# Two accumulators instead of one in the 31-tap depthwise convolution of the last block

## What is computed

```python
D_MODEL, SEQ, CONV_WIDTH, D_CONV_2 = 2048, 512, 31, 1024

def conformer_conv(glu_a, glu_b, conv_w, conv_b, ln_g, ln_b, w_pw, b_pw):
    u = glu_a * jax.nn.sigmoid(glu_b)
    u = lax.conv_general_dilated(
        u, conv_w.reshape(CONV_WIDTH, 1, D_CONV_2).astype(u.dtype),
        window_strides=(1,), padding=[(CONV_WIDTH - 1, 0)],
        dimension_numbers=('NWC', 'WIO', 'NWC'), feature_group_count=D_CONV_2) + conv_b
    u = jax.nn.silu(layer_norm(u, ln_g, ln_b))
    return u @ w_pw + b_pw
```

## Time and profile before

| | before |
|---|---|
| median of 3 runs | 3659.15 us (3657.35 to 3663.39) |
| profiled execution, its own time | 3659.0 us |
| span of its profile | 3657.4 us |
| PE, DVE, ACT, POOL busy | 94%, 60%, 36%, 6% of the span |
| line 1844 (taps 1 to 30), x240 | 180.5 us busy, 752 ns each, 35.9 us idle before |
| stretch 2822 to 3110 us | PE 263.7 us busy, DVE 249.3 us, granted PE clock 0.96 of full |

### The profile page before, as it was taken

How to read it: one execution, slowest core, us unless ns; L and a number is a source line. 1 busy time by engine, 2 the same in 40 slices (tenths; PEclk the granted TensorE clock), 3 DMA queues, 4 the chain that set the end, 5 groups by cost and what they waited for, 6 DMA issues and landing times.

```text
span 3657.4 us, 48550 instructions
## 1 busy us (share of the span) xinstructions
PE 3419.7 (94%) x16800; PEld 2707.4 (74%) x16800; DVE 2195.0 (60%) x2852; ACT 1319.3 (36%) x1757; POOL 210.7 (6%) x396
## 2 busy tenths in 40 slices
PE   8699998899999999998799999999998998998996
PEld 2299998678777777788688777777875777787784
DVE  6455545787676764666564565655655888444433
ACT  0144553432344433325522344443226212344323
POOL 1000000001000000110010000000110000000000
PEclk9799999999999999998899999999999999999998
DMA  9844445445222321654454233322652222221231
GB/s 379 278 161 170 164 152 212 150 169 204 109 100 106 106 98 72 230 208 145 178 205 173 104 112 108 108 96 72 222 191 93 91 80 92 78 78 63 101 120 66
DMA packets 95164, 516.32 MB, mean 141 GB/s; under 512 B 11536, under 2 KB 11568, under 8 KB 55760
## 3 DMA queue, kind: packets, MB, share of 16 engines
q1 hardware_dynamic: 51328, 343.95, 25.8%
q0 software_dynamic: 43728, 170.91, 13.6%
HBM read 492.80 MB, written 22.02 MB: 141 GB/s over the span
## 4 chain that ended last, share of the span: by engine, by line
PE 69%; DVE 13%; DVEq 5%; ACT 4%; issue 4%; DMA 4%; ACTq 1%; SPq 0%; POOL 0%; POOLq 0%; PEldq 0%
PE acc L995 19%; PE acc L997 19%; PE acc L996 19%; DVE xy L1844 5%; PE pv L1075 2%; DVE w_lo L1372 2%; PE S L1056 2%; DVEq L1843 2%; DVE gates L1419 2%; PE S L1234 2%; DVEq L1408 2%; PE misc L1216 1%; ACT w_hi L540 1%; PE S L1064 1%; ACT h_hi L540 1%
## 5 line engine op out<-in xcount | busy, mean ns | idle before, releaser
L995 PE MATMUL acc<-h_hi,w_hi 128*128 128x512 f32 (+1 forms) x4736 | 1752.6, 370 | 140.0 <-DVE h_lo L1378 67.3
L997 PE MATMUL acc<-h_hi,w_lo 128*128 128x512 f32 (+1 forms) x4736 | 1712.8, 362 | 0.0
L996 PE MATMUL acc<-h_lo,w_hi 128*128 128x512 f32 (+1 forms) x4736 | 1712.5, 362 | 0.0
L995 PEld LDWEIGHTS acc<-h_hi,w_hi 128*128 128x128 f32 x4736 | 909.1, 192 | 330.0 <-issue 121.8
L997 PEld LDWEIGHTS acc<-h_hi,w_lo 128*128 128x128 f32 x4736 | 909.3, 192 | 135.4
L996 PEld LDWEIGHTS acc<-h_lo,w_hi 128*128 128x128 f32 x4736 | 910.7, 192 | 130.8 <-issue 6.7
L1372 DVE TENSOR_TENSOR w_lo<-raw,w_hi 128x2048 fp32r<-128x2048 f32 x296 | 677.7, 2290 | 434.1 <-ACT w_hi L540 427.7
L540 ACT ACTIVATE w_hi<-raw 128x2048 fp32r<-128x2048 f32 x296 | 565.0, 1909 | 7.6 <-DVEq L1363 6.2
L540 ACT ACTIVATE ev<-acc 128x512 f32<-128x512 f32 (+1 forms) x210 | 111.1, 533 | 977.3 <-PE acc L997 951.9
L1419 DVE SCALAR_TENSOR_TENSOR gates<-gates,csil 128x512 f32<-128x512 f32 x568 | 412.4, 750 | 78.5 <-DMA gates<-in_wm 42.2
L540 ACT ACTIVATE work<-S,small 128x768 f32<-128x768 f32 (+1 forms) x160 | 129.2, 814 | 276.4 <-DVE small L1509 276.4
(11 more groups left out here) (199 smaller groups left out, 2053.4 us busy)
## 6 DMA issues: line engine op xcount, KB each, us to landing
raw<-in_w SPq DMA_DIRECT2D x296, 1024.0 KB, 4.8
gates<-in_wm POOLq DMA_DIRECT2D x216, 512.0 KB, 4.5
xy<-in_wm SPq DMA_DIRECT2D x32, 1024.0 KB, 9.9
x_d<-xy POOLq DMA_DIRECT2D x2, 4096.0 KB, 13.6
vtok<-in_wm POOLq DMA_DIRECT2D x8, 512.0 KB, 7.1
qb<-x_d POOLq DMA_DIRECT2D x16, 256.0 KB, 3.1
kb<-x_d POOLq DMA_DIRECT2D x16, 256.0 KB, 3.7
out_y<-xy POOLq DMA_DIRECT2D x4, 1024.0 KB, 4.1
```

What stands on the lines that cost most here:

```text
L995: mm(o, w_hi[:, w], h_hi[:, x], start=n == 0, stop=False)
L996: mm(o, w_hi[:, w], h_lo[:, x], start=False, stop=False)
L997: last = mm(o, w_lo[:, w], h_hi[:, x], start=False, stop=n == len(ks) - 1)
```

## The change

Even taps add to `u`, odd taps to `t2` (tap 1 starts it with a plain multiplication). A drain stands ahead of every even tap but tap 0, so that a pair (even, odd) runs between two drains. At the end, behind a drain, `t2` is added to `u`, and the rest is as before. The split of the taps is now 10, 10 and 11.

```diff
-            TAP_PARTS = (range(0, 11), range(11, 21), range(21, TAPS))
+            TAP_PARTS = (range(0, 10), range(10, 20), range(20, TAPS))
 
             def taps(c, part):
 
                 u = tile(xy, c + 8, SEQ)
                 for tap in TAP_PARTS[part]:
+                    x, w = work[:, tap:tap + SEQ], vec("dw", c * TAPS + tap)
+                    if tap % 2 == 0 and tap:
+                        dve.drain()
                     if tap == 0:
-                        ts(u, work[:, 0:SEQ], vec("dw", c * TAPS), vec("dw_b", c), ALU.mult, ALU.add)
+                        ts(u, x, w, vec("dw_b", c), ALU.mult, ALU.add)
+                    elif tap == 1:
+                        ts(t2[:], x, w, None, ALU.mult)
                     else:
-                        dve.drain()
-                        stt(u, work[:, tap:tap + SEQ], vec("dw", c * TAPS + tap), u, ALU.mult, ALU.add)
+                        to = (u, t2[:])[tap % 2]
+                        stt(to, x, w, to, ALU.mult, ALU.add)
                 if part == 2:
+                    dve.drain()
+                    tt(u, u, t2[:], ALU.add)
                     dve.drain()
                     tt(t1[:], t1[:], u, ALU.add)
                     dve.drain()
```

## The result

The changed kernel takes 3637.11 us (median of 4 runs, 3635.45 to 3639.11) against 3659.93 for the kernel before, measured beside it (4 runs); the ratio is 0.9937, 95% interval 0.992 to 0.9955. So 22.8 us went, where 23.4 were forecast; the interval of the ratio allows 16.5 to 29.3. The time lies in the range.

A forecast was written before the change was run, and what follows sets the result against it. DVE was taken as the bound of the taps. Six channel tiles in the loop at 3.28 us (19.7) and two outside at 1.87 (3.7) give 23.4 us off 3659.0: 3635.6 us, range 3631 to 3645.

The forecast's parts named there:

- What bounds: From 2822 to 3112 us DVE is the bound: 37.35 us a channel tile against 32.64 for PE's three tiles.
- Second tap of a pair: Undrained odd tap starts 0.67 us after the even one; 14 pairs save 3.54 us a channel tile in the loop.
- Rival 1: Register step exposed inside a pair in the loop: undrained pitch 0.75 us, time 3644.5 us; chance 0.10.
- rival 2: Second tap of each pair still waits for the whole of the first: 4.1 us slower, 3663.1; chance 0.03.
- rival 4: Something in the edit lengthens the drained pitch by 0.06 us for 15 pairs in the loop: 3641 us; chance 0.05.
- Taps 0 and 1: From tap 0 to tap 2 in the loop, 1.65 us becomes 1.13, a gain of 0.52.
- The added sum: Drain and addition of t2 into u at each channel tile's end, a cost of 0.78 us.
- The sum: Gain of 3.28 us a channel tile in the loop, 1.87 outside it, 23.4 us together.
- gap of 1.43 us: In the loop, DVE's new beat of 34.07 us against PE's 32.64: DVE still the bound, PE idle about 1.3.
- rival 3: PE becomes the bound if its clock falls after a 1.3 us wait: three tiles 34.44 us, time 3637.8; chance 0.08.
- What comes behind: After the last sum: PE still waits some 7 us before mean, and the 547 us to the end are kept.
- The drain rule: The skill's rule that no operation starts until the pipeline empties, so the edit removes nothing; the trace speaks against it.

The follow-up runs named there:

- e2: The kernel before with only the new tap split (10/10/11), one accumulator and all drains; 3662.82 us against 3662.64, ratio 1.0002.
- e5: The changed kernel with taps 16 to 30 left out, parts of 6, 6 and 4 taps; 3619.41 us, ratio 0.9880.
- e3: The changed kernel with three accumulators, a drain ahead of every third tap and two sums at the end; 3632.92 us, ratio 0.9921.
- e1: The changed kernel with a drain again ahead of every tap but tap 0; 3668.52 us, ratio 1.0017.
- e4: The changed kernel with the sum into t1 put behind the GLU product of the next channel tile; 3635.43 us, ratio 0.9927.
- e6: The changed kernel with three accumulators and the sum into t1 behind the GLU product; 3628.45 us, ratio 0.9904.
- e7: As e6, with the layer norm's mean moved into PE's fourth tile of kv2; 3624.22 us, ratio 0.9899.

## Why the prediction was right

The mechanism was right in each of its parts, as the trace shows below. That the median came within 0.6 us of the forecast gain is partly luck, since the time alone has an interval of 16.5 to 29.3 us; the stretch, which is measured much more closely, gained 24.85.

- *What bounds.* Right: DVE sets the beat. The e2 kernel moves PE's waits about and the beat doesn't move; e5 shows where PE takes over, at 32.63 (32.64 worked out).
- *Second tap of a pair.* Right at 0.67, in the loop as outside; the register step is hidden, as line 1692 had said. Rival 1 (0.75) and rival 2 (0.92) are out. The drain ahead of the even tap costs what it did, 0.92 (rival 4 is out).
- *Taps 0 and 1.* 2859.25 to 2860.38 is 1.13, as worked out.
- *The added sum.* Its step to the next is 0.77 (2887.80 to 2888.57), worked out 0.78; writing through a register address cost nothing more.
- *The sum.* A beat fell by 3.48 us where 3.28 were worked out, and the first and last channel tile by 1.97 and 1.99 (to the next `lo`, or to the last sum) instead of 1.87. Together 24.85 against 23.4. The term that was short is the gain in the loop, by 0.20 a beat: a pair takes 1.583 us (three from 2860.38 to 2865.13), not 1.593, which makes 0.14 in 14 pairs, and the mean beat before held some 0.08 of issue gaps (37.35 against 37.27 from 2853.95 to 2891.22).
- *PE.* A gap of 1.43 us was worked out from start to start, it is 33.87 - 32.64 = 1.23; the idle time 0.85 to 1.02 instead of 1.3. The granted clock stayed at 1.00 over the loop, so rival 3 is out; by its own sum it would have cost 2.2 us.
- *What comes behind.* Right: PE waits 6.4 us for the last sum (some 7 said) and the rest takes as long as it did. The last sum was said to start at 3086.7 and started at 3090.36, because the taps themselves began 5.07 us later.
- *The drain rule (rival 2).* The Trainium skill, "VectorE: DVE Perf Modes", section "The DRAIN you can't avoid", has the next operation wait until the pipeline is empty and says that this can't be skipped by leaving out semaphores. The prediction took this as a rule against the edit and left out a sentence of the same section, "A next op that is not held starts earlier"; by the section that it points to, an operation is held when its operands start in another group of 32 partitions than those ahead. All tiles of the taps have 128 partitions, so no tap is held by it, and the page as a whole speaks for the gain. The trace agrees with that part: with no drain of the program between them, operations of 0.75 us start every 0.67 us, three in a row in e3. The same page's rule for chained operations is to lower their count. Here more operations were faster: with taps and sums counted, the kernel before has 32 a channel tile, the changed one 33 and e3 34, and the stretches are 288.24, 263.39 and 258.38 us.

## What to carry to other kernels

A chain of dependent operations on one engine costs its drains only where that engine sets the beat; find that from the chain of waits of the stretch, not from the busy share of the span, where DVE had 60%. There, split the chain over as many accumulators as pay for their final sums, and put independent work behind a drain that must stand. Work out beforehand where the next engine takes over: here 1.2 us a beat further, after which the rest of the gain was behind the loop, in a wait that went when the waiting instruction was moved.

## What the runs showed that I had not expected

- Single operations of DVE come late, with nothing in the profile to wait for, and these gaps are not random. In the loop of the kernel before it is tap 14 of the second channel tile in each of the three passes, 0.36 us late in the first pass and 0.12 in the two others (0.53 and 0.29 idle, where 0.17 is usual):

```profile
2908.70 0.75 DVE L1844 SCALAR_TENSOR_TENSOR xy<-work,vecs,xy 128x512 f32 x1 [0.53 <-issue]
...
2983.32 0.75 DVE L1844 SCALAR_TENSOR_TENSOR xy<-work,vecs,xy 128x512 f32 x1 [0.29 <-issue]
```

  e2 has them at the same tap, though its split moved it among the `lo`; e1 and e4 have two places a pass (up to 0.2 us a beat), e3 has one at a sum, and the changed kernel, e6 and e7 have none at a tap of their loops. So the places go with the instructions of the kernel. What sets them was not tried.
- The start of the taps, behind code that is the same in all these kernels, varies by 5.7 us between executions (2821.3 to 2827.0), a quarter of the gain measured. A stretch between two instructions of the same execution came back to 0.1 us in the one repeat there is, where the whole time needs several runs to tell 5.
